# Whole-tile turns, sample-memory products on two row halves and memories decayed ahead by POOL in a hybrid recurrent decoder step

## The chip, the cores and the metric

The kernel runs on one core of one Trainium2 chip. The metric is device time in microseconds for one launch, which computes the whole two-layer trunk; the figure for a kernel is the median of its runs. One more execution is recorded by the hardware profiler, and all rows below come from that one.

## What is computed

Each of two layers is: a SwiGLU feed-forward half step with a layer norm, one input projection, two recurrent mixers side by side, an output projection with a layer norm, and a second feed-forward half step. A prompt of 256 tokens and 8 samples of 8 tokens share the weights; only the samples come with states. Cut to the state updates that the change touches:

```python
def step(S, inp):                       # RWKV-7, 8 heads of 64x64, per token
    r_t, w_t, k_t, v_t, kk_t, a_t = inp
    sa = jnp.einsum('bhvk,bhk->bhv', S, -kk_t)
    S = (S * w_t[:, :, None, :] + sa[..., None] * (kk_t * a_t)[:, :, None, :]
         + v_t[..., None] * k_t[:, :, None, :])
    return S, jnp.einsum('bhvk,bhk->bhv', S, r_t)
...
C = dec[..., None, None] * C + jnp.einsum('bhs,bhsd,bhse->bhde', ws, kc, vc)   # mLSTM, 4 heads of 128x128, per chunk
n = dec[..., None] * n + jnp.einsum('bhs,bhsd->bhd', ws, kc)
```

## The kernel before

Everything is kept transposed: features on the 128 partitions, the 320 tokens (two tiles of 128 prompt tokens and tile 2 of 64 sample tokens) along the free dimension. The projections and feed-forward parts split each fp32 weight and activation in a high and a low fp32r part and make three products of them (`three_passes`, L2047 to L2049); weights come by SP's queue into four slots `raw`, ScalarE makes the high part (L2337) and VectorE the low one (L2538). Engines meet only by semaphores, and the order of the work on each engine is written out by hand.

The mixers stand between the input and the output projection. `tensor_mixers` first turns the mLSTM keys and values to tokens on partitions, tile by tile (`keys_of_tile`, L535; `values_of_tile`, L544; ScalarE copies them with `copy_keys`, L1049, and `copy_values`, L1057), between the RWKV score products (L755). Then comes the growth loop of 27 steps (`for n in range(NSTEP)`), which inverts a triangular matrix for each of 5 RWKV chunks in up to 6 levels. A step, called by its n below, is: a product on TensorE (L725), a mask on VectorE (L1660), the two growth products of the step before (L737, L740), a copy on ScalarE (L1133). Everything else of the mixers is hung on these steps by lists of numbers:

- `SIDE_AT`: the side jobs of `side`, which all go through bank 7 and are each copied out by ScalarE in `copy_side` before the next may start: the last rows, the values of 5 chunks (L665), the keys of 5 chunks in two halves each (L674, 10 sides at steps 9 to 18), three products for the right-hand sides (L681), the convolution ends (L685), and four turns of wkv memories (L694, steps 23 to 26).
- `NUM_AT`, `SCORES_AT`, `HEAD_AT`: the mLSTM's products of a tile; head statistics on VectorE at steps 17, 18 and 20 for tiles 0 and 1, at 24 to 26 for tile 2 (L1471 to L1510).
- `LEFT_AT`: the left-over jobs in banks 4 to 6. The eight C jobs are the new sample memories, each the half (4 samples) of one head: TensorE multiplies keys of tile 2 with the values masked by sample (L630, 512 columns), and VectorE multiplies the old memory by its decay and adds the product, four instructions per job (L1522). They stand in pairs at steps 20, 21, 23 and 24. Their masked values come from POOL (L1828), in two buffers. The sample memories lie in `raw` and leave on SP's queue (L2029) before the output projection's weights may come in.

POOL's queue in this stretch is, in order: identity added to the scores (L1859), the decayed keys `bkh` (L1864, L1867), zeroing of `qm` (L1873), the load of wkv memories (L1877), decay matrices (L1881), masked values (L1828), memory terms (L1836), and two groups of stores. Behind the loop stands `recurrence`, four chunks in sequence.

The pattern of a left-over and a side job in the code:

```python
if kind == "C":
    pe.wait_ge(vmask_ready.sem, vmask_ready.by(L, i // 2 + 1))
    last = pe.matmul(b[:, :], kt[0:TS, 2, i // 2, :], vmask[(i // 2) % 2][:, 4 * (i % 2):4 * (i % 2) + 4, :],
                     start=True, stop=True)
```

## Time and profile before

| | |
|---|---|
| median of 3 runs | 1550.63 us (1549.57 to 1556.33) |
| span of the profiled execution | 1551.5 us |
| VectorE busy | 982.2 us (63%) |
| ScalarE busy | 696.5 us (45%) |
| POOL busy | 375.1 us (24%) |
| mean granted TensorE clock | 0.975 |
| growth loop and recurrence, layer 1 | about 389 to 500 us |
| the same, layer 2 | about 1147 to 1265 us |

A granted clock of 1.00 is 2.4 GHz, 0.50 is 1.2 GHz. PE is TensorE, DVE VectorE, ACT ScalarE. A matmul in fp32 leaves more than one record. Neighbouring records of one line are merged in a timeline, so that a group's duration runs from its first start to its last end, with an end that may overlap the next group's start. L12 is line 12 of the kernel before.

### The profile page before, as it was taken

How to read it: one execution, taken by the hardware profiler on the slowest of the kernel's cores; microseconds unless marked ns; L12 is line 12 of the kernel's file. 1: busy time of each engine (PE TensorE's matmuls, PEld its weight loads, DVE VectorE, ACT ScalarE, POOL GpSimd, SP SyncE). 2: the span in 40 equal slices, each digit the busy share in tenths (PEclk: the TensorE clock that was granted, in tenths of full speed). 3: DMA queues.
4: the chain of work that ended last, by engine and by line, in shares of the span. 5: the costliest groups of instructions: out<-in, count | busy, mean ns of one | idle time of the engine just before them, and what ended most of it. 6: DMA issues, size and time to landing. Idle time of an engine off the chain costs nothing.

```text
span 1551.5 us, 34978 instructions
## 1 busy us (share of the span) xinstructions
PE 1489.7 (96%) x13874; PEld 1434.4 (92%) x13874; DVE 982.2 (63%) x1571; ACT 696.5 (45%) x1198; POOL 375.1 (24%) x395
## 2 busy tenths in 40 slices
PE   7999998999889999999999999989988999999995
PEld 7999998999778999999999999989988789999995
DVE  4444445587276787776577775466944667877644
ACT  4333334755545543334343334367563355333332
POOL 4222472011241422221322221200142304222100
PEclk9999999999998999999999999999999799999998
DMA  8555542553123655444545545534430434545451
GB/s 216 149 149 149 165 149 69 136 137 96 32 60 91 167 157 154 137 148 136 169 138 147 149 149 164 149 96 109 109 85 3 120 86 143 170 138 164 144 163 34
DMA packets 318846, 198.89 MB, mean 128 GB/s; under 512 B 7696, under 2 KB 303664, under 8 KB 318736
## 3 DMA queue, kind: packets, MB, share of 16 engines
q1 hardware_dynamic: 315120, 190.69, 42.2%
q0 software_dynamic: 3616, 6.62, 2.0%
q8 instruction: 82, 1.34, 0.4%
q14 instruction: 28, 0.23, 0.0%
HBM read 188.50 MB, written 8.78 MB: 127 GB/s over the span
## 4 chain that ended last, share of the span: by engine, by line
PE 83%; DVE 8%; ACT 5%; DVEq 2%; issue 2%; DMA 0%; ACTq 0%; SPq 0%
PE bank L2047 23%; PE bank L2049 23%; PE bank L2048 23%; DVE wlo L2538 2%; PE bank L2134 1%; PE bank L630 1%; PE bank L725 1%; ACT whi L2337 1%; DVE rlo L2569 1%; PE bank L2139 1%; PE bank L455 1%; ACT z L1133 1%; PE bank L740 1%; PE bank L755 1%; PE bank L737 1%
## 5 line engine op out<-in xcount | busy, mean ns | idle before, releaser
L2337 ACT ACTIVATE whi<-raw 128x1024 fp32r<-128x1024 f32 x340 | 358.8, 1060 | 470.3 <-PE bank L2049 453.9
L2538 DVE TENSOR_TENSOR wlo<-raw,whi 128x1024 fp32r<-128x1024 f32 x340 | 421.7, 1244 | 228.5 <-ACT whi L2337 227.7
L2047 PE MATMUL bank<-rhi,whi 128*128 128x322 f32 x984 | 306.5, 311 | 0.0
L2049 PE MATMUL bank<-rhi,wlo 128*128 128x322 f32 x984 | 305.9, 311 | 0.0
L2048 PE MATMUL bank<-rlo,whi 128*128 128x322 f32 x984 | 304.8, 310 | 0.0
L2047 PE MATMUL bank<-xh,whi 128*128 128x320 f32 x912 | 285.3, 313 | 5.8 <-DVE xl L2712 3.5
L2048 PE MATMUL bank<-xl,whi 128*128 128x320 f32 x912 | 282.2, 309 | 0.0
L2049 PE MATMUL bank<-xh,wlo 128*128 128x320 f32 x912 | 282.2, 309 | 0.0
L2807 POOL TENSOR_TENSOR hl<-scratch,hh 128x320 f32 x88 | 146.8, 1668 | 496.4 <-DVE scratch L2659 379.7
L2047 PE MATMUL bank<-hh,whi 128*128 128x320 f32 (+1 forms) x704 | 218.4, 310 | 0.5 <-DVE wlo L2538 0.5
L2048 PE MATMUL bank<-hl,whi 128*128 128x320 f32 (+1 forms) x704 | 217.4, 309 | 0.0
L2049 PE MATMUL bank<-hh,wlo 128*128 128x320 f32 (+1 forms) x704 | 217.4, 309 | 0.0
L2048 PEld LDWEIGHTS bank<-rlo,whi 128*128 128x128 f32 x984 | 186.5, 189 | 0.0
L2047 PEld LDWEIGHTS bank<-rhi,whi 128*128 128x128 f32 x984 | 185.5, 189 | 0.0
L2049 PEld LDWEIGHTS bank<-rhi,wlo 128*128 128x128 f32 x984 | 185.5, 189 | 0.0
L2047 PEld LDWEIGHTS bank<-xh,whi 128*128 128x128 f32 x912 | 172.1, 189 | 10.9 <-issue 7.2
L2048 PEld LDWEIGHTS bank<-xl,whi 128*128 128x128 f32 x912 | 172.2, 189 | 0.5
L2049 PEld LDWEIGHTS bank<-xh,wlo 128*128 128x128 f32 x912 | 172.1, 189 | 0.0
L2047 PEld LDWEIGHTS bank<-hh,whi 128*128 128x128 f32 x704 | 132.3, 188 | 1.4 <-issue 1.0
L2048 PEld LDWEIGHTS bank<-hl,whi 128*128 128x128 f32 x704 | 132.4, 188 | 0.2
L2049 PEld LDWEIGHTS bank<-hh,wlo 128*128 128x128 f32 x704 | 132.4, 188 | 0.0
L2640 DVE TENSOR_TENSOR scratch<-bank,scratch 128x322 f32<-128x322 f32 x132 | 64.9, 491 | 70.8 <-PE bank L2049 63.1
(411 smaller groups left out, 1960.3 us busy)
## 6 DMA issues: line engine op xcount, KB each, us to landing
raw<-in_ffn_wg SPq DMA_DIRECT2D x88, 512.0 KB, 3.8
raw<-in_ffn_wu SPq DMA_DIRECT2D x88, 512.0 KB, 3.8
raw<-in_ffn_wd SPq DMA_DIRECT2D x88, 512.0 KB, 3.7
raw<-in_w_in SPq DMA_DIRECT2D x60, 512.0 KB, 3.8
raw<-in_w_out SPq DMA_DIRECT2D x16, 512.0 KB, 6.4
raw<-in_state_C SPq DMA_DIRECT2D x8, 512.0 KB, 6.2
out_s_C<-raw SPq DMA_DIRECT2D x8, 512.0 KB, 3.8
ring<-in_state_wkv POOLq DMA_DIRECT2D x2, 1024.0 KB, 8.3
```

What stands on the lines that cost most here:

```text
L455: return pe.matmul(out, src, ident[0:rows, 0:rows], start=True, stop=True)
L630: last = pe.matmul(b[:, :], kt[0:TS, 2, i // 2, :], vmask[(i // 2) % 2][:, 4 * (i % 2):4 * (i % 2) + 4, :], start=True, stop=True)
L725: last = pe.matmul(bank[n % 2][PART[1 - q], j * CH:(j + 1) * CH], ati[part, c, j, :], xi(q, c, j), start=True, stop=True)
L737: pe.matmul(bank[2 + q][PART[q], j * CH:(j + 1) * CH], xti(q, c, j), t1[PART[1 - q], c, j, :], start=True, stop=True)
L740: last = pe.matmul(bank[2 + q][PART[1 - q], j * CH:(j + 1) * CH], t1[PART[1 - q], c, j, :], xti(q, c, j), start=True, stop=True)
L2047: pe.matmul(out, w_hi, hi, start=start, stop=False)
L2048: pe.matmul(out, w_hi, lo, start=False, stop=False)
L2049: return pe.matmul(out, w_lo, hi, start=False, stop=stop)
L2337: act.activation(whi[:, slot, :], raw[:, slot, :], ACT.Copy).then_inc(hi_ready.sem, 1)
L2538: dve.tensor_tensor(wlo[:, slot, :], raw[:, slot, :], whi[:, slot, :].bitcast(F32), ALU.subtract).then_inc(lo_ready.sem, 1)
L2640: dve.tensor_tensor(scaled, bank_of(L, f, d)[:, 0:T + 2], root, ALU.mult)
L2807: pool.tensor_tensor(at(hl), hval[:, k % 2, :], at(hh).bitcast(F32), ALU.subtract).then_inc(hl_done.sem, 1)
```

## The change

- The second head of each pair gets a second copy of its keys, values and gate column of tile 2, on partitions 64 to 127. The C jobs are reordered so that the two of a step belong to the two heads of a pair; one uses rows 0 to 63 of TensorE, the other rows 64 to 127.
- The old sample memories are multiplied by their decay on POOL (`decayed_memory`, eight instructions), and VectorE only adds the product, one instruction per C job, behind a new wait on `memory_decayed`. The masked values are made for two heads at once, so that two POOL instructions stay of four.
- The keys of a chunk are turned as full tiles, four transpositions for a chunk, in one side instead of two; POOL therefore writes the two kinds of decayed keys in swapped places on the upper partitions, in eight instructions instead of three.
- The wkv memories are loaded with two heads beside each other, in four DMAs of POOL's queue instead of one, and turned by four transpositions of full tiles per side instead of sixteen products of 64x64.
- With 5 sides fewer, `SIDE_AT` puts the keys at steps 9, 10, 11, 13, 14, the products for right-hand sides at 15 to 17, the ends at 19, and the wkv memories at 20, 21, 23 and 24.

The diff, with context cut:

```diff
...
         tail = area(6144, P, rows=(SB + 1) * NRW, of=ring)
-        wkv_rows = area(6144, SB, NJ, NA, of=ring)
+        wkv_rows = area(6144, SB, NJ // 2, P, of=ring)
         C0 = raw[:, :, :].rearrange("p h (b e) -> p h b e", b=SB)
...
         hsq = area(0, 2 * HB * DK, of=spare)
-        vmask = [area(1536, SB, DK, rows=TS, of=spare), area(15304, SB, DK, rows=TS)]
+        vmask = [area(1536, SB, DK, of=spare), area(15304, SB, DK)]
...
         h_ready = signal("h_ready", 2)
-        vmask_ready = signal("vmask_ready", HB)
+        memory_decayed = signal("memory_decayed", 2 * HB)
+        vmask_ready = signal("vmask_ready", HB // 2)
         left_mm = signal("left_mm", 13)
...
         x_copied = signal("x_copied", NSTEP)
-        side_mm = signal("side_mm", 24)
-        side_copied = signal("side_copied", 24)
+        side_mm = signal("side_mm", 19)
+        side_copied = signal("side_copied", 19)
         tail_out = signal("tail_out", 32)
         ends_left = signal("ends_left", 48)
-        wkv_in = signal("wkv_in", 16)
+        wkv_in = signal("wkv_in", 64)
         samples_mm = signal("samples_mm", 4)
...
                     last = turn(pe, bank[4][0:rows, (n * 3 + q) * HB:(n * 3 + q + 1) * HB], row[:, q, at:at + rows])
+            for h in range(0, HB, 2):
+                own = 8 * HB + h
+                last = pe.matmul(bank[4][PART[1], own:own + 1], row[:, 2, 2 * P:T], sel[:, h + 1, 0:1],
+                                 start=True, stop=True)
             last.then_inc(cols_turned.sem, 1)
...
                 last = turn(pe, bank[4 + n][0:rows, h * DK:(h + 1) * DK], qk[:, HB + h, at:at + rows])
+                if n == 2 and h % 2 == 0:
+                    last = turn(pe, bank[4 + n][PART[1], h * DK:(h + 1) * DK], qk[:, HB + h + 1, at:at + rows])
             last.then_inc(kv_turned.sem, 1)
...
         def values_of_tile(pe, L, n):
...
                                     ident[:, :])
+                if n == 2 and h % 2 == 0:
+                    last = pe.matmul(bank[5][PART[1], h * DK:(h + 1) * DK], mv[:, h + 1, at:at + rows], ident[:, :],
+                                     start=True, stop=True)
             last.then_inc(kv_turned.sem, 1)
...
         def tile_scores(pe, L, n):
...
             if kind == "C":
-                pe.wait_ge(vmask_ready.sem, vmask_ready.by(L, i // 2 + 1))
-                last = pe.matmul(b[:, :], kt[0:TS, 2, i // 2, :], vmask[(i // 2) % 2][:, 4 * (i % 2):4 * (i % 2) + 4, :],
+                g, half, q = i // 4, i // 2 % 2, i % 2
+                pe.wait_ge(vmask_ready.sem, vmask_ready.by(L, g + 1))
+                last = pe.matmul(b[:, :], kt[PART[q], 2, 2 * g, :], vmask[g][PART[q], 4 * half:4 * half + 4, :],
                                  start=True, stop=True)
...
-        VALUES, KEYS, RVS, ENDS, MEMS = 1, 1 + NCH, 1 + 3 * NCH, 4 + 3 * NCH, 5 + 3 * NCH
+        VALUES, KEYS, RVS, ENDS, MEMS = 1, 1 + NCH, 1 + 2 * NCH, 4 + 2 * NCH, 5 + 2 * NCH
         NSIDE = MEMS + SB // 2
-        SIDE_AT = [*range(KEYS), *range(KEYS + 3, NSIDE + 3)]
+        SIDE_AT = [*range(KEYS), 9, 10, 11, 13, 14, 15, 16, 17, 19, 20, 21, 23, 24]
+        assert len(SIDE_AT) == NSIDE
         RV = ((0, 1), (2, 3), (NPC,))
...
         def side(pe, L, k):
...
                     pe.wait_ge(bkh_ready.sem, bkh_ready.by(L, 1))
-                c, q = (k - KEYS) // 2, (k - KEYS) % 2
                 for j in range(NJ):
-                    for kind in range(2):
-                        last = pe.matmul(b[PART[q ^ kind], j * NA:(j + 1) * NA], bkh[PART[q], j, c, kind, :],
-                                         ident[PART[q], PART[q]], start=True, stop=True)
+                    last = pe.transpose(b[:, j * P:(j + 1) * P],
+                                        bkh[:, j, k - KEYS, :, :].rearrange("p s t -> p (s t)"), ident[:, :])
             elif k < ENDS:
...
                 if k == MEMS:
-                    pe.wait_ge(wkv_in.sem, wkv_in.by(L, 16))
+                    pe.wait_ge(wkv_in.sem, wkv_in.by(L, 64))
                 for i in range(2):
-                    for j in range(NJ):
-                        for part in PART:
-                            at = (i * NJ + j) * NA
-                            last = pe.matmul(b[part, at:at + NA], wkv_rows[part, 2 * (k - MEMS) + i, j, :],
-                                             ident[part, part], start=True, stop=True)
+                    for jj in range(NJ // 2):
+                        at = (i * NJ // 2 + jj) * P
+                        last = pe.transpose(b[:, at:at + P], wkv_rows[:, 2 * (k - MEMS) + i, jj, :], ident[:, :])
             last.then_inc(side_mm.sem, 1)
...
                 last = act.activation(cols[0:rows, n, 1:3, :], src[:, 1:3, :], ACT.Exp)
+            last = act.activation(cols[PART[1], 2, 2, 0:HB:2], bank[4][PART[1], 8 * HB:9 * HB:2], ACT.Exp)
             last.then_inc(cols_ready.sem, 1)
...
                                       scale=cols[0:rows, n, 2, h:h + 1])
+            if n == 2:
+                for h in range(0, HB, 2):
+                    last = act.activation(kt[PART[1], 2, h, :], bank[6][PART[1], h * DK:(h + 1) * DK], ACT.Identity,
+                                          scale=cols[PART[1], 2, 2, h:h + 1])
             last.then_inc(kv_ready.sem, 1)
...
         def copy_values(act, L, n):
...
             act.wait_ge(kv_turned.sem, kv_turned.by(L, NTT + n + 1))
+            if n == 2:
+                act.activation(va[PART[1], 2, 0:HB:2, 0:DK],
+                               bank[5][PART[1], :].rearrange("p (h d) -> p h d", h=HB)[:, 0:HB:2, :], ACT.Copy)
             act.activation(va[0:rows, n, :, 0:DK], bank[(7, 4, 5)[n]][0:rows, :].rearrange("p (h d) -> p h d", h=HB),
...
             elif k < RVS:
-                c, q = (k - KEYS) // 2, (k - KEYS) % 2
-                last = act.activation(bkt[c][:, :, q, :], heads4(b), ACT.Copy)
+                last = act.activation(bkt[k - KEYS][:, :, :, :].rearrange("p j q n -> p (j q n)"), b[:, :], ACT.Copy)
             elif k < ENDS:
...
             if kind == "C":
-                h, half = i // 2, i % 2
-                for k in range(4):
-                    s = 4 * half + k
-                    at = h * TS + s * ST + ST - 1
-                    last = dve.scalar_tensor_tensor(out=C0[:, h, s, :], in0=C0[:, h, s, :], scalar=rexp[:, at:at + 1],
-                                                    in1=b[:, k * DK:(k + 1) * DK], op0=ALU.mult, op1=ALU.add)
+                h, half = 2 * (i // 4) + i % 2, i // 2 % 2
+                own = C0[:, h, 4 * half:4 * half + 4, :].rearrange("p b e -> p (b e)")
+                dve.wait_ge(memory_decayed.sem, memory_decayed.by(L, i + 1))
+                last = dve.tensor_tensor(own, own, b[:, :], ALU.add)
             elif kind == "H":
...
-        def masked_values(pool, L, h):
-
-            values = va[0:TS, 2, h, 0:DK].rearrange("t (o e) -> t o e", o=1)
-            own = bmask[0:TS, :].rearrange("t (b o) -> t b o", o=1)
-            pool.tensor_tensor(vmask[h % 2], bcast(values, 1, SB), bcast(own, 2, DK),
+        def masked_values(pool, L, g):
+
+            values = va[:, 2, 2 * g, 0:DK].rearrange("t (o e) -> t o e", o=1)
+            own = bmask[:, :].rearrange("t (b o) -> t b o", o=1)
+            pool.tensor_tensor(vmask[g], bcast(values, 1, SB), bcast(own, 2, DK),
                                ALU.mult).then_inc(vmask_ready.sem, 1)
+
+        def decayed_memory(pool, L, i):
+
+            h, half = 2 * (i // 4) + i % 2, i // 2 % 2
+            own = C0[:, h, 4 * half:4 * half + 4, :]
+            at = h * TS + 4 * half * ST
+            decay_ = rexp[:, at:at + 4 * ST].rearrange("p (b t) -> p b t", t=ST)[:, :, ST - 1:ST]
+            pool.tensor_tensor(own, own, bcast(decay_, 2, DK), ALU.mult).then_inc(memory_decayed.sem, 1)
...
         def memory_term(pool, L, j):
...
             two = lambda t: t.rearrange("p j c s t -> p j c (s t)")
-            pool.tensor_tensor(two(bkh[:, :, 0:NPC, :, :]), two(bk[:, :, 0:NPC, :, :]),
-                               bcast(dlast[:, :, 0:NPC].rearrange("p j (c o) -> p j c o", o=1), 3, 2 * CH), ALU.mult)
             for s in range(2):
-                last = pool.tensor_tensor(
-                    seqs(bkh[:, :, NPC, s, :]), seqs(bk[:, :, NPC, s, :]),
-                    bcast(dlast[:, :, NPC:NPC + SB].rearrange("p j (c o) -> p j c o", o=1), 3, ST), ALU.mult)
+                pool.tensor_tensor(bkh[PART[0], :, 0:NPC, s, :], bk[PART[0], :, 0:NPC, s, :],
+                                   bcast(dlast[PART[0], :, 0:NPC].rearrange("p j (c o) -> p j c o", o=1), 3, CH),
+                                   ALU.mult)
+                pool.tensor_tensor(bkh[PART[1], :, 0:NPC, s, :], bk[PART[1], :, 0:NPC, 1 - s, :],
+                                   bcast(dlast[PART[1], :, 0:NPC].rearrange("p j (c o) -> p j c o", o=1), 3, CH),
+                                   ALU.mult)
+                for q, part in enumerate(PART):
+                    last = pool.tensor_tensor(
+                        seqs(bkh[part, :, NPC, s, :]), seqs(bk[part, :, NPC, s ^ q, :]),
+                        bcast(dlast[part, :, NPC:NPC + SB].rearrange("p j (c o) -> p j c o", o=1), 3, ST), ALU.mult)
             last.then_inc(bkh_ready.sem, 1)
...
             carry(pool)
-            dma(wkv_rows[:, :, :, :].rearrange("p b j k -> p (b j) k"),
-                lay(I["state_wkv"]).rearrange("l b (j q) v k -> (q v) (l b j) k", q=2)).then_inc(wkv_in.sem, 16)
+            for a, part in enumerate(PART):
+                for q in range(2):
+                    src = lay(I["state_wkv"]).rearrange("l b (j h) v k -> v (l b j) h k", h=4)
+                    dma(wkv_rows[part, :, :, q * NA:(q + 1) * NA].rearrange("p b j k -> p (b j) k"),
+                        src[:, :, 2 * a + q, :]).then_inc(wkv_in.sem, 16)
             pool.wait_ge(tile_mm.sem, tile_mm.by(L, NTT))
...
             pool.wait_ge(num_mm.sem, num_mm.by(L, NTT))
+            decayed_memory(pool, L, 0)
+            decayed_memory(pool, L, 1)
             masked_values(pool, L, 1)
-            pool.wait_ge(left_mm.sem, left_mm.by(L, 2))
-            masked_values(pool, L, 2)
-            pool.wait_ge(left_mm.sem, left_mm.by(L, 4))
-            masked_values(pool, L, 3)
+            for i in range(2, 2 * HB):
+                decayed_memory(pool, L, i)
             pool.drain()
...
                 for h in range(HB):
-                    sp.wait_ge(left_done.sem, left_done.by(L, LEFT.index(("C", 2 * h + 1)) + 1))
+                    sp.wait_ge(left_done.sem, left_done.by(L, LEFT.index(("C", 4 * (h // 2) + 2 + h % 2)) + 1))
                     sp.dma_start(lay(O["s_C"])[:, :, h, :, :].rearrange("l b d e -> d (l b) e"),
```

## Rows read from the trace of the kernel before

**Rows 1.** The page: busy time, share of the span and instructions of each engine.

```profile
PE 1489.7 (96%) x13874; PEld 1434.4 (92%) x13874; DVE 982.2 (63%) x1571; ACT 696.5 (45%) x1198; POOL 375.1 (24%) x395
```

**Rows 2.** The page: shares by engine of the chain that ended last.

```profile
PE 83%; DVE 8%; ACT 5%; DVEq 2%; issue 2%; DMA 0%; ACTq 0%; SPq 0%
```

**Rows 3.** Windows: stretch, length, PE, PEld, DVE, ACT, POOL busy, clock, DMA, GB/s.

```profile
391.00:433.00 42.00, 36.07 (x984) 33.46 (x984) 12.45 (x38) 21.75 (x64) 11.82 (x10) 0.92 0.13 29
433.00:443.00 10.00, 7.18 (x262) 6.49 (x259) 9.39 (x21) 2.76 (x8) 4.73 (x2) 1.00 0.01 3
443.00:466.00 23.00, 21.46 (x482) 15.54 (x474) 17.21 (x60) 10.75 (x27) 9.64 (x7) 1.00 0.35 99
...
1191.00:1201.00 10.00, 7.26 (x256) 6.57 (x252) 9.04 (x21) 3.06 (x9) 4.94 (x2) 1.00 0.02 6
1201.00:1231.00 30.00, 29.39 (x482) 20.73 (x482) 17.84 (x60) 10.58 (x27) 8.24 (x7) 0.72 0.26 75
```

**Rows 4.** Timeline of TensorE: start, duration, line, records, idle before.

```profile
281.88 1.35 PE L487 MATMUL bank<-scratch 64*128 64x320 f32 x8
...
354.64 2.16 PE L455 MATMUL bank<-ident,scratch 32*128 32x32 f32 x20
...
381.14 1.09 PE L455 MATMUL bank<-ident,scratch 128*64 128x128 f32 x8
382.15 0.66 PE L544 MATMUL bank<-ident,scratch 128*128 128x128 f32 x4
...
432.50 0.68 PE L674 MATMUL bank<-ident,spare 64*64 64x64 f32 x16
...
442.77 0.27 PE L737 MATMUL bank<-spare,z 64*64 64x64 f32 x2 [2.82 <-DVE spare L1660]
...
443.30 1.10 PE L681 MATMUL bank<-scratch 64*64 64x64 f32 x32
444.90 1.98 PE L630 MATMUL bank<-spare,ring 64*128 64x512 f32 x4 [0.50 <-ACT ring L1083]
...
453.54 1.10 PE L694 MATMUL bank<-ident,ring 64*64 64x64 f32 x32
```

**Rows 5.** The chain of waits, first layer, ahead of the growth loop: start, us, what.

```profile
385.47 0.57 PE bank L544 x4
386.06 0.60 ACT ring L1057
```

**Rows 6.** Timeline of ScalarE.

```profile
382.26 1.13 ACT L1049 ACTIVATE ring<-bank,scratch 64x128 f32<-64x128 f32 x4 [0.31 <-PE bank L455]
...
444.07 0.77 ACT L1083 ACTIVATE ring<-bank 64x258 f32<-64x258 f32 x2
```

**Rows 7.** Timeline of POOL.

```profile
390.88 3.61 POOL L1864 TENSOR_TENSOR spare<-scratch 128x2048 f32<-128x2048 f32 x1 [0.35 <-issue]
394.45 1.22 POOL L1867 TENSOR_TENSOR spare<-scratch 128x256 f32<-128x256 f32 x2
...
439.00 2.88 POOL L1828 TENSOR_TENSOR scratch<-ring,bmask 64x1024 f32<-64x1024 f32 x1
...
452.59 2.05 POOL L1836 TENSOR_TENSOR scratch<-scratch,bmask 128x512 f32<-128x512 f32 x2 [0.24 <-ACT scratch L1120]
```

**Rows 8.** One line, L674: ns min/median/max, first and last start in us.

```profile
L674 PE MATMUL bank<-ident,spare x320: 218/218/365, 406.7 to 1194.5; 64*64 64x64 f32 x160
```

**Rows 9.** Timeline of VectorE.

```profile
435.96 1.17 DVE L1482 TENSOR_TENSOR ring<-ring,scratch 128x1024 f32<-128x1024 f32 x1
...
437.55 2.57 DVE L1492 TENSOR_TENSOR spare<-ring 128x1024 f32<-128x1024 f32 x1
...
448.06 2.15 DVE L1522 SCALAR_TENSOR_TENSOR raw<-raw,ring,bank 128x128 f32<-128x128 f32 x8
...
452.86 1.28 DVE L1528 TENSOR_TENSOR scratch<-bank,scratch 128x512 f32<-128x512 f32 x2
```

**Rows 10.** The chain of waits, second layer, step 20.

```profile
1203.44 3.75 PE bank L630 x4
```

## The prediction

> **What bounds the kernel now.** I read the page first: TensorE is busy for 96% of the span [rows 1] and holds 83% of the chain that ended last [rows 2]. The reader should see that most of this is the projections and feed-forward layers, which the change leaves alone. The change lives in the mixer stretch, some 120 us per layer, so I cut that stretch into windows [rows 3]. From 391 to 433 us TensorE is busy 36 of 42 us at a granted clock of 0.92: steps 5 to 17 of the growth loop. From 433 to 443 VectorE is busy 9.39 of 10 us and TensorE 7.18: VectorE's head means and squares set the pace. From 443 to 466 both are loaded (21.5 and 17.2 of 23 us). The second layer is the same but for its last part, which takes 30 us at a clock of 0.72 where the first takes 23 us at 1.00. So what an edit is worth depends on its step; I went through it by the timelines of the four engines [rows 4, 6, 7, 9] and by the chain of waits [rows 5, 10] and asked at each step which wait ends last.
>
> **The change, part by part.** One record of an ordinary fp32 matmul counts half of that matmul; a transposition of a full tile is one record only [rows 4]: eight records for four products at L455, four for four transpositions at L544.
>
> (1) Second copy of keys, values and gate columns. Before the growth loop TensorE turns keys of tile 2 (four products of 64 tokens, 1.01 us from the start of L455 to that of L544 [rows 4]), so 0.25 us each. Two more for keys and two more for values are 1.0 us, and they stand in the unbroken TensorE work ahead of the last values copy, which the chain runs through [rows 5]. Behind it ScalarE has one more copy of 64 rows before its table load; ScalarE copies of 64 rows by 256 to 258 take 0.38 (two L1083 in 0.77) [rows 6]. The two added key copies cost 0.28 each (four L1049 in 1.13) [rows 6] and are hidden by ScalarE's waits for values; uncovered they would be 0.56. The two gate-column products lie in the input projection, TensorE-bound: the twenty records of such small products take 2.16 us (L455 at 354.64) [rows 4], four are 0.43. Sum: 1.0 + 0.38 + 0.43 = 1.8 us **lost** per layer.
>
> (2) POOL's decayed keys. One instruction over 2048 elements takes 3.61 us and two small ones 1.22 [rows 7]. By its elements each of the four new ones over 1024 takes 1.8, so 7.2, and the small ones double to 2.4: 4.8 us later, at 400.5 instead of 395.7. The first turn of keys starts at 406.7 [rows 8], so 6 us of cover remain. Behind them on POOL's queue stand the zeroing of qm and now four issues of wkv memories instead of one; they are needed at steps 16 and 20, the latter at 443 (L681) [rows 4], over 35 us later. I cost this at nothing; if the cover were gone, up to 5 us per layer.
>
> (3) Turns of keys. Ten sides of eight products (0.68 for one, L674) become five sides of four transpositions (0.66, L544) [rows 4]; some 0.1 of each is a tail that overlaps the next work. TensorE saves five times 0.57, 2.9 us, but nearly none on the path. The removed sides leave steps 12, 14 and 18, where TensorE waits for ScalarE's and VectorE's weights of a tile anyway; step 15 gets a product side (sixteen products, L681, 1.10 [rows 4]) in place of a turn, and it does stand ahead of the next product: 0.4 us, and 0.6 at the clock of 0.92 and lower that this window has: 0.6 us **lost** per layer. The like at step 16 is hidden behind VectorE.
>
> (4) Turns of wkv memories. Four sides of sixteen products (1.10, L694) become four transpositions each (0.66, L544) [rows 4]: 0.44 saved four times, two of them where TensorE sets the pace.
>
> (5) Products into the sample memories. A pair takes 1.98 us [rows 4] (L630, four records of 0.495). In the changed kernel the two of a pair use different row halves and banks. The row that shows such a pattern is L487: eight records of 320 columns with alternating row halves in 1.35 us [rows 4]. At 0.495 x 320/512 = 0.31 each they would need 2.5 us one after another, so they ran two at a time. I take 1.0 us for a pair, bounds 1.0 and 1.98.
>
> (6) VectorE. Eight instructions of a pair take 2.15 us (L1522); two additions over 512 elements from PSUM and SBUF take 1.28 (L1528, same form) [rows 9]: 0.87 saved per pair.
>
> (7) POOL's decays. Eight over 128x512 at about 1.02 (two L1836 in 2.05 [rows 7]), and two masks fewer. From about 438, where its masks begin now (the second runs from 439.00), POOL has two decays, one mask of 1.8 (half of L1864's 3.61 for half its elements) and six decays without a wait: 10.0 us, until some 448.5. The first pair's products end at 444.9 + 1.0, when two decays have long been done; each later pair comes 2 us or more behind it, as long as POOL takes for two. So no wait on memory_decayed is expected. But POOL is now busy through 438 to 448.5, and the rows show that the two engines hold each other up: L1482 takes 1.17 us, L1492 of the same size, beside a POOL mask, 2.57, and the mask beside it 2.88 [rows 7, 9]. The additions of (6) read one operand from PSUM, as L1522 did, and no L1522 row is stretched. I take 0.5 us lost at the first head scaling, half of one POOL instruction; L1492 might win back up to 1.4 if POOL starts behind it, which I leave out. Bounds: -1.4 and +2 per layer. The Trainium skill, GPSIMD Engine Reference, the table at its head, says that POOL shares its SBUF interfaces with VectorE and contends with VectorE instructions that have two SBUF inputs; by that rule, the trace agrees (2.57 against 1.17).
>
> Steps 20 to 24 of the first layer, from the sum of these: step 20 starts from ScalarE's table load and is VectorE-bound: -0.87 + 0.5 = -0.4. Step 21: VectorE, -0.85. Step 23: TensorE-bound, 1.98 + 1.10 become 1.0 + 0.66, then VectorE binds: -1.2. Step 24: VectorE (head means, then the pair), -0.85. Steps 22, 25, 26: nothing. Together **-3.3 us**. In the second layer the first two pairs run at half clock, 3.75 us for the first on the chain [rows 10]: a pair saves 1.85 there. Two of them are -3.7, and -1.5 remains of the other steps: **-5.2 us**.
>
> (8) Changes of tile shape. Turns with full tiles stand between products of 64x64; before they had the same shape. The Trainium skill, TensorEngine Tiling (Array Packing), Key Properties, says that a change of tiling mode drains TensorE. This rule speaks against the change. No row isolates its price. Without that rule a bound from rows: the 64x64 work before L544 and behind it leaves no gap in the windows where TensorE is full, so I take nothing, and as upper end for the nine sides the 0.1 us tail of each, 0.9 us per layer.
>
> **Sum.** Layer 1: +1.8 +0.6 -3.3 = -0.9. Layer 2: +1.8 +0.6 -5.2 = -2.8. Together -3.7 us. The profiled execution's span is 1551.5, 0.9 above the median 1550.63; against the median I forecast 1546.9.
>
> **Rivals.** *Half clock in the first layer too* (the slower side). VectorE-bound steps 17 to 19 leave TensorE idle for 2.82 us (L737) [rows 4]; the change takes turns out of just these steps, so it idles longer. In the first layer the clock stayed, in the second it fell behind such a gap [rows 3]. The first layer's 23 us would become as the second's 30: 6.8 lost, 1.9 of it given back by cheaper pairs, 4.9 net: 1551.8. (Full clock is 2.4 GHz, half is 1.2.) It decides once it costs over 3.7 us, if the fall comes before step 22. For it: the same program has both cases in one execution. Against: the gap grows by 1 or 2 us only. Chance 0.22.
> *Clock kept in the second layer*: the mirror image, 1546.9 - 4.9 = 1542.0; chance 0.15.
> *The pairs don't overlap*: then (5) gives nothing, steps 23 and 24 lose 0.4, the second layer 3.7: 1551.0. Against it stands L487; chance 0.08.
> *POOL's decays hold VectorE up*: each POOL instruction of 1.02 us can stand ahead of the two head products and scalings of tiles 0 and 1, at most 2 us a layer: 1550.9; chance 0.12. By the skill's rule on shared interfaces it is these instructions, with two SBUF inputs, that would be longer.
> *The forecast*: 0.43.
>
> **Numbers.** The clock rivals and the bounds of (7) and (8) set the range, 1540.5 to 1555. A measurement here can tell about 0.5%, 7.75 us, from no change: faster means below 1542.9, slower above 1558.4. Faster 0.20 (most of the clock-kept case, with part of the forecast's lower tail); slower 0.06 (clock fallen and POOL's holding together, or an unseen drop later in the mixer); the same 0.74.
>
> **What would show it.** Right: L630 pairs of about 1.0 us; L1522 gone, additions of 0.64; L674-like turns as records of 128x128, four each; the last values copy 1.4 us later against the start of the stretch; POOL's last decay ended before the third pair of additions; the first layer's stretch from step 19 to 26 about 20 us instead of 23.3. Wrong: a VectorE wait on POOL before an addition; TensorE waiting for wkv rows at step 20 or for bkh at step 9; a pair of 1.5 to 2 us; a low clock at a place where it was full, which would move the total by more than all my terms together.

## The result

The changed kernel takes 1562.87 us (median of 7 runs, 1558.99 to 1566.81), the kernel before 1553.25 beside it (7 runs, 1549.57 to 1557.27): ratio 1.0065, 95% interval 1.0047 to 1.0083. It is 0.65% **slower**; the forecast was 1546.9 us, 0.2% faster, with a range that ended at 1555.

The page after, as [rows 1, 2]: busy time by engine, then the shares of the chain that ended last.

```profile
span 1559.3 us, 34012 instructions
PE 1485.8 (95%) x13394; PEld 1428.9 (92%) x13394; DVE 986.7 (63%) x1523; ACT 696.0 (45%) x1196; POOL 395.1 (25%) x423
PE 84%; DVE 7%; ACT 5%; DVEq 2%; issue 1%; DMA 0%; SPq 0%; ACTq 0%
```

TensorE does 4 us less work and the span is 7.8 longer. VectorE has 48 instructions fewer and is 4.5 us busier: some of them got longer. POOL has 20 us more. From the first score product to the first weight split of the output projection (`wlo`) the two layers take 119.8 and 126.6 us before, 126.1 and 127.7 after: +7.4 of the 7.8. By stage, from the places of the growth masks:

| stage | layer 1, us | layer 2, us |
|---|---|---|
| ahead of the first mask behind the score products | +1.33 | +1.34 |
| from there to the mask of step 18 | +0.02 | +2.55 |
| mask of step 18 to mask of step 19 (step 19 below) | +2.07 | +2.21 |
| mask of step 19 to mask of step 26 | +0.39 | -6.12 |
| from there to `wlo` (the recurrence) | +2.52 | +1.16 |

Windows of after, as [rows 3] (stretch, length, PE, PEld, DVE, ACT, POOL busy, granted clock, DMA, GB/s):

```profile
391.00:433.00 42.00, 35.12 (x955) 31.85 (x957) 12.34 (x37) 23.48 (x64) 20.00 (x20) 0.96 0.15 30
433.00:443.00 10.00, 7.13 (x225) 6.01 (x216) 9.54 (x19) 2.86 (x10) 4.86 (x4) 1.00 0.04 10
443.00:446.00 3.00, 0.00 (x0) 0.00 (x0) 2.85 (x4) 0.00 (x0) 3.00 (x4) 0.71 0.06 16
446.00:470.00 24.00, 19.13 (x321) 13.24 (x321) 17.17 (x37) 9.41 (x23) 8.78 (x9) 0.78 0.28 79
470.00:492.00 22.00, 20.98 (x380) 19.48 (x384) 8.93 (x23) 7.38 (x19) 5.40 (x8) 0.50 0.43 122
```

Two things are new. TensorE does nothing at all from 443 to 446 us while VectorE and POOL are both full; and the clock, which before was 1.00 from 443 to 466, is here 0.71 in that gap (it falls inside it), 0.78 from 446 to 470 and 0.50 until 492.

**The gap.** VectorE before, the statistics ahead of the mask of step 19, which follow L1492 (2.57 us) [rows 9] and L1494:

```profile
441.48 0.41 DVE L1496 SCALAR_TENSOR_TENSOR scratch<-scratch 128x8 f32<-128x8 f32 x1
441.97 0.17 DVE L1498 TENSOR_TENSOR scratch<-scratch 128x8 f32<-128x8 f32 x1
442.22 0.17 DVE L1500 TENSOR_SCALAR scratch<-scratch 128x8 f32<-128x8 f32 x1
```

The same five instructions after, and the masks behind them:

```profile
439.04 2.10 DVE L1507 TENSOR_TENSOR spare<-ring 128x1024 f32<-128x1024 f32 x1
441.22 1.22 DVE L1509 TENSOR_REDUCE scratch<-spare 128x8 f32<-128x1024 f32 x1
442.51 1.42 DVE L1511 SCALAR_TENSOR_TENSOR scratch<-scratch 128x8 f32<-128x8 f32 x1
444.00 0.93 DVE L1513 TENSOR_TENSOR scratch<-scratch 128x8 f32<-128x8 f32 x1
445.01 0.93 DVE L1515 TENSOR_SCALAR scratch<-scratch 128x8 f32<-128x8 f32 x1
445.86 0.74 DVE L1673 TENSOR_TENSOR spare<-bank,lvmask 128x256 f32<-128x256 f32 x2
...
451.23 1.99 DVE L1525 TENSOR_TENSOR ring<-ring,scratch 128x1024 f32<-128x1024 f32 x1
```

And POOL and TensorE of after:

```profile
439.01 3.04 POOL L1850 TENSOR_TENSOR raw<-raw,ring 128x512 f32<-128x512 f32 x2 [5.14 <-PE bank L619]
442.01 1.89 POOL L1841 TENSOR_TENSOR scratch<-ring,bmask 128x1024 f32<-128x1024 f32 x1
443.87 6.07 POOL L1850 TENSOR_TENSOR raw<-raw,ring 128x512 f32<-128x512 f32 x6
450.09 2.04 POOL L1857 TENSOR_TENSOR scratch<-scratch,bmask 128x512 f32<-128x512 f32 x2 [0.16 <-issue]
```

```profile
446.32 0.37 PE L745 MATMUL bank<-spare,z 64*64 64x64 f32 x2 [5.47 <-DVE spare L1673]
```

Two instructions over 8 elements a partition take 0.93 us in place of 0.17, nearly the length of one decay (six in 6.07). Their ends fall on the ends of POOL's instructions: L1511 ends at 443.93, where POOL's mask makes way for a decay (443.87), L1513 at 444.93 and L1515 at 445.94, and decays follow each other about every 1.01 us from 443.87 on. Against before, L1507 is 0.47 shorter, L1511 is 1.01 longer, L1513 and L1515 0.76 each: +2.06, and from one growth mask (L1673) to the next this step takes 7.16 instead of 5.09 us, +2.07 (7.15 instead of 4.94 in the second layer). TensorE waits for those masks for 5.47 us where it waited 2.82 [rows 4].

**The half clock.** By windows of 1 us in the two mixer stretches, TensorE is at 0.50 in before from 410, 427 and 468 us, the last until 482, and in the second layer also from 1202 to 1219: 51 us together. In after it is so from 427, 444 and 468, the last until 492: 75 us together.

Such a sum is of one execution, and it scatters. In e4 and e12 below, whose instructions are those of after as far as the loop's step 20, it is 14 us between 376 and 438 us, in after itself 3. A difference of some 10 us between two kernels is therefore not read from one trace alone. The mean clock of all runs of a kernel says more. The kernel before, run more than 130 times beside the experiments, took 1557.9 us on average in the 19 runs at a mean clock of 0.972 and 1549.6 in the 10 at 0.978: 18.6 us less of half clock over the whole program go with 8.3 us less time, 0.45 us for each. Where TensorE is not what the others wait for, half clock costs less (e4 below).

### The profile page after: what moved, and what is told of

Its sections match the earlier page's. It is cut to its first block, busy times and chain, and to the rows that moved or that the text cites. A ratio compares the mean times of both kernels' runs of the same rounds, so it can differ in the third digit from the quotient of the medians.

```text
span 1559.3 us, 34012 instructions
## 1 busy us (share of the span) xinstructions
PE 1485.8 (95%) x13394; PEld 1428.9 (92%) x13394; DVE 986.7 (63%) x1523; ACT 696.0 (45%) x1196; POOL 395.1 (25%) x423
## 3 DMA queue, kind: packets, MB, share of 16 engines
q8 instruction: 78, 1.28, 0.4%
## 4 chain that ended last, share of the span: by engine, by line
PE 84%; DVE 7%; ACT 5%; DVEq 2%; issue 1%; DMA 0%; SPq 0%; ACTq 0%
PE bank L2076 23%; PE bank L2078 23%; PE bank L2077 23%; DVE wlo L2567 2%; PE bank L2163 1%; ACT whi L2366 1%; DVE rlo L2598 1%; PE bank L733 1%; PE bank L456 1%; PE bank L2168 1%; ACT z L1148 1%; PE bank L641 1%; PE bank L745 1%; PE bank L748 1%; PE bank L788 1%
```

## The experiments

Theory A: POOL's decays hold up VectorE's statistics; taken away, the loss goes. Theory B: TensorE's clock falls behind idle time, and part of the loss comes from that. A filler below is a TensorE product whose result nobody reads. The runs are in this table, each ratio against runs of the kernel before on the same chip (so it is not the quotient of the two medians); mean clock is that of all runs of the kernel, which over the whole program makes 3.1 us of half clock for each 0.001; half clock is the sum over 1 us windows of 2 x (1 - granted clock) in both stretches, step 19 the distance from its growth mask back to the one before it, first and second layer, these two from one profiled execution each.

| kernel | median us | ratio to before | interval | mean clock | half clock us | step 19 us |
|---|---|---|---|---|---|---|
| before | 1553.25 | 1 | | 0.974 | 51 | 5.09, 4.94 |
| after | 1562.87 | 1.0065 | 1.0047 to 1.0083 | 0.968 | 75 | 7.16, 7.15 |
| e1 decays late | 1553.97 | 0.9998 | 0.9983 to 1.0012 | 0.970 | 72 | 3.49, 3.80 |
| e2 decays on VectorE | 1558.03 | 1.0019 | 1.0001 to 1.0038 | 0.970 | 68 | 5.61, 5.26 |
| e3 turns only | 1561.98 | 1.0042 | 1.0026 to 1.0059 | 0.967 | 82 | 5.22, 4.87 |
| e4 filler in after | 1564.28 | 1.0058 | 1.0037 to 1.0079 | 0.970 | 72 | 7.16, 7.16 |
| e5 products only | 1554.48 | 1.0007 | 0.9989 to 1.0026 | 0.975 | 44 | 7.61, 7.62 |
| e6 filler in before | 1547.29 | 0.9961 | 0.9942 to 0.9980 | 0.978 | 41 | 5.09, 4.94 |
| e7 e1, second term late | 1553.38 | 1.0001 | 0.9983 to 1.0019 | 0.970 | 65 | 3.49, 3.79 |
| e8 turns, old places | 1552.29 | 0.9998 | 0.9985 to 1.0011 | 0.971 | 75 | 5.05, 4.63 |
| e9 e7, later places | 1555.66 | 1.0021 | 1.0008 to 1.0035 | 0.969 | 79 | 3.84, 4.20 |
| e10 products, late decays | 1549.24 | 0.9974 | 0.9958 to 0.9990 | 0.978 | 51 | 4.84, 5.15 |
| e11 e10 and filler | 1549.98 | 0.9987 | 0.9971 to 1.0003 | 0.977 | 55 | 4.84, 5.15 |
| e12 after, filler at end | 1560.48 | 1.0040 | 1.0024 to 1.0057 | 0.976 | 55 | 7.15, 7.15 |
| e13 before, two fillers | 1542.07 | 0.9932 | 0.9911 to 0.9954 | 0.987 | 17 | 5.08, 4.94 |
| e14 e10, two fillers | 1548.00 | 0.9960 | 0.9944 to 0.9976 | 0.983 | 38 | 4.84, 5.16 |
| e15 e7, two fillers | 1548.77 | 0.9978 | 0.9963 to 0.9993 | 0.983 | 24 | 3.49, 3.80 |
| e16 before, small fillers | 1543.70 | 0.9917 | 0.9896 to 0.9939 | 0.984 | 31 | 5.09, 4.95 |

### Decays behind the statistics (e1, e7), and on VectorE (e2)

```diff
# e1, and e7
             pool.wait_ge(num_mm.sem, num_mm.by(L, NTT))
+            pool.wait_ge(hvar_ready.sem, hvar_ready.by(L, 1))
             decayed_memory(pool, L, 0)
# e7 beside it
-            pool.wait_ge(left_mm.sem, left_mm.by(L, 10))
+            pool.wait_ge(left_done.sem, left_done.by(L, 10))
# e2
-                last = dve.tensor_tensor(own, own, b[:, :], ALU.add)
+                (four scalar_tensor_tensor per job, as in the kernel before; no decays on POOL)
```

> The changed kernel with one more wait: POOL starts its decays of the sample memories only when VectorE has finished the head statistics of tiles 0 and 1 (signal hvar_ready). Theory A (collision): in the changed kernel POOL's back-to-back decays hold up the short VectorE instructions of step 18 (1.42, 0.93 and 0.93 us where the kernel before has 0.41, 0.17, 0.17), and t1 of step 18 to t1 of step 19 takes 7.15 us against 5.1. By A this distance falls back to 5.1 or below in both layers, TensorE's gap falls from 5.4 to about 3.3 us, and the time falls by at least 4 us: ratio to the kernel before 1.001 to 1.004. Theory B (clock): what costs is the low clock behind a TensorE gap, and the gap is mostly the removed TensorE work; then the gap stays above the 2.8 us of before, the clock still falls behind it in both layers, and the ratio stays at 1.005 to 1.007. Theory C (added work ahead of the loop and product sides at step 15): nothing to do with POOL, ratio stays at 1.0065.

> The changed kernel with the decays back on VectorE (four instructions a job, as before), everything else changed. Theory A (collision): step 18 to 19 back at 5.1 us; the later steps lose the 0.87 us per pair that the additions saved, but win back the stretched statistics of tile 2; ratio 1.000 to 1.003. Theory B (clock): gap still longer than before, ratio about 1.005. Theory C (added copies, product side at step 15): ratio about 1.005, with +1.4 and +0.6 us per layer ahead of step 17 unchanged.

> As e1 (decays start behind the statistics of tiles 0 and 1), and POOL's second memory term waits until VectorE has made the last memory addition, so that it doesn't run beside the statistics of tile 2 in step 24. Theory A (collision): step 25 falls from 5.36 us to about 3.8, as VectorE's instructions there sum up without being held; 1 to 1.5 us per layer, ratio 0.998 against 0.9998 for e1. Theory B (clock): the shorter steps are given back by TensorE at low clock behind them: ratio as e1, 1.000.

e1 takes back the whole 0.65%. VectorE in e1, in the same place, with POOL's first decay at 443.83:

```profile
440.44 1.22 DVE L1507 TENSOR_TENSOR spare<-ring 128x1024 f32<-128x1024 f32 x1
441.73 1.22 DVE L1509 TENSOR_REDUCE scratch<-spare 128x8 f32<-128x1024 f32 x1
443.02 0.17 DVE L1511 SCALAR_TENSOR_TENSOR scratch<-scratch 128x8 f32<-128x8 f32 x1
443.27 0.17 DVE L1513 TENSOR_TENSOR scratch<-scratch 128x8 f32<-128x8 f32 x1
443.51 0.17 DVE L1515 TENSOR_SCALAR scratch<-scratch 128x8 f32<-128x8 f32 x1
```

All five have their lone length, L1507 too, which in before is held up by a POOL mask. Nothing but one wait on POOL was added, so the collision is the cause of these 3.67 us (7.16 to 3.49). The wait holds back POOL's second mask too, which stands behind the first two decays. So 2.07 of the 3.67 are what after had lost against before, and 1.6 are a holding that before has as well: e1 gains more than it undoes (its forecast by Theory A was 1.001 to 1.004), and that its ratio is 1 does not mean that the decays were the whole loss. Over both layers after lost 4.3 us in step 19, of 9.6. The expensive instructions are the three over 8 elements: none is long, each waits for a POOL instruction. e2 leaves POOL's early mask in place and lies between: L1507 takes 2.94 us, L1511 0.56, the head scaling 1.23 where after has 1.99. e7 takes the same collision out of step 25 too, 5.37 to 3.79 us, and its ratio does not move beyond its interval: step 26 takes 3.56 us in place of 2.83, and TensorE stands 2.88 us ahead of the last growth products.

### Each half of the change (e5, e3, e8)

```diff
# e5: after, with before's turns and SIDE_AT.  e3: before, with after's turns and SIDE_AT.  e8: e3 and
-        SIDE_AT = [*range(KEYS), 9, 10, 11, 13, 14, 15, 16, 17, 19, 20, 21, 23, 24]
+        SIDE_AT = [*range(KEYS), 9, 10, 11, 13, 14, 19, 20, 21, 22, 23, 24, 25, 26]
```

> The kernel before with the whole-tile turns of keys and wkv memories alone (new order of side jobs, swapped writes of POOL, four DMAs); no second copies, no row halves, decays on VectorE. Theory A (collision): masks of POOL meet VectorE as before; only +0.6 us at step 15 and -0.4 to -0.9 us at the late turns per layer: ratio 0.998 to 1.000. Theory B (clock): TensorE has 3 us less work per layer around step 18, its gap grows from 2.8 to about 3.5 to 4.5 us, the clock falls in both layers, ratio 1.002 to 1.004. Theory C says the turns' side at step 15 costs: at most 1.001.

> The kernel before with the sample-memory products alone: second copies of keys and values, two heads on the two row halves, decays ahead by POOL, one addition; turns and side jobs as before. Theory A (collision): step 19 takes about 7.1 us instead of 5.1 and step 25 about 5.4, and 1.3 us per layer are added ahead of step 5: with the first layer's pairs saving little, ratio 1.003 to 1.006. Theory B (clock): TensorE keeps its side jobs in steps 19 to 26, so the low clock behind step 24 is shorter than the 24 us of the changed kernel in the first layer, and the ratio is 1.000 to 1.002.

> The kernel before with the whole-tile turns alone, as in e3 (1.0042), but the side jobs behind the keys stay at their old steps: products for right-hand sides at 19 to 21, ends at 22, wkv turns at 23 to 26. Theory D (what cost e3 was the moving of TensorE work ahead of the gap): 1.1 us per layer come back at steps 16 and 17, and the low clock behind the gap in the first layer becomes shorter or goes: ratio 0.999 to 1.001. Rival: the transpositions themselves, with their changes of tile shape, cost: then steps 10 to 14 or 24 to 26 are longer than before and the ratio stays near 1.004.

e3 and e8 do the same work; eight side jobs stand at other steps. e3 is at 1.0042, e8 at 0.9998, and the intervals are apart. The windows from 445 to 462 us show where; first e3, then e8:

```profile
445.00:462.00 17.00, 16.63 (x165) 10.12 (x162) 7.94 (x23) 5.30 (x12) 5.84 (x4) 0.51 0.22 63
```

```profile
445.00:462.00 17.00, 15.93 (x291) 10.29 (x290) 12.29 (x41) 8.05 (x21) 6.89 (x4) 1.00 0.29 81
```

TensorE is equally busy, with half the instructions in e3, at 0.51. Ahead of that it had stood 3.55 us in e3 (ahead of the growth products behind the masks of steps 19 and 20) and 2.28 and 0.57 in e8. From the mask of step 19 to that of step 26 e3 takes 30.03 and 26.32 us, e8 22.97 and 22.63. So whole-tile turns have no price of their own that shows (0.9998), and the price of their places is for the most part the clock: 0.967 against 0.971 in the mean, though by the half-clock sums the two differ by only 7 us. e8's half clock from 435 to 443 lies where VectorE sets the pace, e3's from 444 to 462 where TensorE is busy throughout. e5, with a step 19 of 7.6 us, is level with before, which Theory A alone does not give; its profiled execution (44 us of half clock, 1550.12 us) is faster than its median by 4.4, so the 44 against 51 says little, and its mean clock is that of before. What it gains are the steps 20 to 26, 21.47 and 21.48 us against 23.28 and 30.13. The two halves, 1.0042 and 1.0007, add to 1.0049 where the whole is 1.0065; the intervals allow that.

### Products whose result nobody reads (e4, e6)

```diff
                     product(pe, L, n)
+                    if n == 20:
+                        for _ in range(6):      # e6: range(3), in the kernel before
+                            pe.matmul(bank[5][:, 0:6 * CH], ident[:, :], lvmask[...], start=True, stop=True)
```

> The changed kernel with six extra TensorE products of 384 columns into an unused part of bank 5 at step 20, where TensorE sits idle for 5.4 us; their result is not used. They take about 0.74 us each, 4.4 in all, so they fit the gap. Theory B (clock): the granted clock stays at 2.4 GHz behind the gap, the first two pairs of memory products and the turns between take half as long, and the time falls by 2 to 6 us, ratio 1.002 to 1.005. Theory A (collision): the gap itself stays, the time falls by at most 1 to 2 us. If the clock falls all the same, ratio unchanged at 1.0065.

> The kernel before with three extra TensorE products of 384 columns at step 20 (about 0.74 us each, unused), in the gap of 2.8 us that TensorE has there. Theory B (clock is bought by TensorE's gaps): the second layer's low clock of 17 us behind that gap does not come or is shorter, and the time falls by 3 to 7 us, ratio 0.996 to 0.998. If the low clock comes whatever TensorE does in the gap: ratio 0.999 to 1.001, and the low stretches only change their places.

e6 only adds work, and it is 0.39% faster. Its first layer is as before; in the second the steps 22 to 24 take 2.40, 1.53 and 3.74 us where before has 5.96, 4.22 and 4.69. In windows, first e6, then (two windows) e13, which has more fillers, against the 0.72 of [rows 3] for the like stretch:

```profile
1201.00:1231.00 30.00, 27.89 (x569) 21.12 (x566) 20.99 (x67) 12.26 (x31) 15.19 (x14) 0.91 0.46 130
```

```profile
468.00:482.00 14.00, 13.18 (x349) 11.04 (x348) 7.24 (x18) 6.42 (x17) 4.88 (x7) 1.00 0.64 174
...
1201.00:1231.00 30.00, 30.00 (x620) 21.94 (x622) 21.40 (x68) 10.97 (x28) 15.05 (x14) 1.00 0.56 152
```

In after the same idea gave nothing (1.0058 beside 1.0065). The six products took 4.14 us and left 1.41 of the 5.47 us idle; the clock stayed at 1.00 until 452 and was low until 456, where in after it is low from 444 to 455. Yet from the mask of step 19 to that of step 26 the first layer takes 23.39 us, and 23.67 in after: this fall, by itself, cost after 0.3 us. The way to the mask of step 21 is as long at either clock (8.48 and 8.47 us); in after VectorE there stands 3.79 us for ScalarE (L1521 for L1112).

### Late places with late decays, and the products alone with them (e9, e10, e11)

```diff
# e9: e7 and
+        SIDE_AT = [*range(KEYS), 9, 10, 11, 13, 14, 18, 19, 20, 21, 22, 23, 24, 25]
# e10: e5 with e7's two waits.   e11: e10 and three products at step 20, as in e6
```

> The changed kernel with GpSimd's decays behind VectorE's statistics and the second memory term late (as in e7_decays_and_term_late), and eight side turns moved from steps 15 to 17 and 19 to 24 to steps 18 to 25. Theory A (only the collision of GpSimd with VectorE costs time; it is gone in e7 at 1.0001): the turns' places are worth nothing, 1.000, steps 16 and 17 a micro-second shorter together and the later ones as much longer. Theory B (a part of the loss is TensorE's clock behind gaps; the two turns-only kernels differ by 0.44% by the places alone): the late places give back the same here, 0.996, and the time at the half clock in both mixer stretches falls from 65 us to about 50.

> The changed kernel without its whole-tile turns (turns and their places as in the kernel before; the pair products, the decays on GpSimd and the one addition stay), with the decays behind VectorE's statistics and the second memory term late. Theory A: the same part without the late decays is at 1.0007 with a step 19 of 7.6 us in both layers; step 19 falls to about 3.5, which is 3.8 us a layer over the stretch at most, so 1551.5 - 7 = 1544.5, 0.9955. Theory B: as in the second layer of the changed kernel, time that is won in front of the gap comes back as half clock behind it; the half-clock time goes up from 44 us, and the ratio is 0.998 to 1.000.

> As e10_products_late_decays, with three TensorE products of 384 columns ahead of step 21 whose result nobody reads (the same three that made the kernel before faster, 0.9961). Theory A: TensorE works 0.5 us more in each layer, so the ratio is that of e10 or up to 0.0006 above it. Theory B: the products keep the clock up behind the gap of step 20, mostly in the second layer, where the three of them were worth 6 us in the kernel before: 0.002 to 0.004 below e10.

e9 missed both ways: late places, worth 0.44% between e3 and e8, gave nothing here (1.0021 beside the 1.0001 of e7; the intervals overlap, so a loss is not shown either). "Later is better" is therefore no rule. e10 is the first version with parts of the change that is faster than both kernels, 0.9974, but by little more than half of what Theory A gave it: step 19 falls to 4.84 and not to 3.5, since its statistics (L1511 at 2.56 us) meet POOL's first mask, and half clock is 51 us, as in before. e11's filler did nothing that the intervals can tell from e10.

### Fillers behind the loop (e12, e13, e16) and with the change's parts (e14, e15)

```diff
+            idle_products(pe, 5)      # e13, e14: 3; e15: 6; e16: 1
             grow(pe, L, NSTEP - 1)
+            idle_products(pe, 2)      # e16: 1
             recurrence(pe, L)
```

`idle_products(pe, k)` makes k of the products of 384 columns, into bank 1. e12 is after with these alone; e13 and e16 are the kernel before, e14 is e10 and e15 is e7, each with the three products at step 20 too.

> The changed kernel with seven TensorE products of 384 columns whose result nobody reads: five ahead of the last half of the growth loop (grow of step 26), where TensorE stands for 2.14 us in the first layer, and two behind it, where it stands for 0.87 us. At some 0.37 us each they fit into the idle time. Theory B (the recurrence is 2.5 us longer in the first layer than before because TensorE is at the half clock from 468 to 492 us, where before it was from 468 to 482, and it is so because TensorE stands 2.0 and 2.1 us in the last steps where it stood 1.1 us): the half clock ends by about 480 or does not come, the stretch from the last growth step to the first output projection falls from 34.8 to 32 us or less, and the ratio is 1.000 to 1.004. Rival: the idle time is not what sets the clock, or other places take it over as with e4_filler: 34.8 us again and 1.0065; if the products are in the way, up to 1.008.

> The kernel before with the three products ahead of step 21 (0.9961 as e6_before_filler) and, beside them, three ahead of grow of step 26 (idle 1.09 us in the first layer) and two behind it (idle 0.87 us). Theory B: the half clock from 468 to 482 us, and that from 1226 to 1239 in the second layer, shrink or go, which is worth up to 6 us a stretch: 0.990 to 0.994. Rival: no further gain, 0.996.

> As e10_products_late_decays (pairs on two row halves, decays on GpSimd behind VectorE's statistics, one addition; the turns as before: 0.9974) with the fillers of e13_before_two_fillers: three products ahead of step 21, three ahead of grow of step 26, two behind it. If what this half of the change wins is real once TensorE stays at full clock: the kernel before with the same fillers is at 0.9932; VectorE has 0.87 us less per pair in steps 20, 21 and 24 and TensorE 0.9 less per pair in step 23, while the copies ahead of the loop cost 1.3 us and step 19 at most nothing, so 1 to 2 us a layer: 0.991 to 0.992. If it only moved idle time: 0.993 or above, with half clock back at another place.

> The whole change with late decays and a late second memory term (as e7_decays_and_term_late, 1.0001) and fillers: three products ahead of step 21, six ahead of grow of step 26 (idle 2.88 us in that kernel), two behind it. Theory B: half clock behind the last growth steps goes, the recurrence falls from 33 or 34 us to 30 or 31, and the ratio is 0.994 to 0.997. If whole-tile turns take so much work out of steps 18 to 26 that the clock falls elsewhere (two turns-only kernels of ours had it behind step 19): 0.998 to 1.001.

> As e13_before_two_fillers (0.9932), with one product ahead of grow of step 26 and one behind it in place of three and two. One such product takes 0.73 us at full clock (six records in 2.20), so three and two of them were longer than the idle times of 1.09 and 0.87 us and held the loop's end up by 1.1 + 0.6 = 1.7 us a layer; one and one fit. If filling the idle time is what keeps the clock: full clock stays, 1.7 us less a layer, 0.991. If it needed that much more work (a rival: the clock answers to how much the products add, not to the idle time they fill): the half clock behind 468 us comes back at least in part, 0.994 to 0.996.

They go against the idle time at the end of the loop. TensorE there, with its idle time in brackets, first before, then after:

```profile
466.05 0.68 PE L740 MATMUL bank<-z,spare 64*64 64x64 f32 x16 [1.09 <-DVE spare L1660]
467.60 0.68 PE L854 MATMUL bank<-scratch,z 64*64 64x64 f32 x16 [0.87 <-ACT z L1133]
```

```profile
467.18 0.68 PE L748 MATMUL bank<-z,spare 64*64 64x64 f32 x16 [2.02 <-DVE spare L1673]
470.00 1.12 PE L748 MATMUL bank<-z,spare 64*64 64x64 f32 x16 [2.14 <-DVE spare L1673]
471.98 1.12 PE L862 MATMUL bank<-scratch,z 64*64 64x64 f32 x16 [0.87 <-ACT z L1148]
```

e12 in the first layer: five products and then two more.

```profile
472.02 5.19 PE L917 MATMUL bank<-lvmask,ident 128*128 128x384 f32 x10
477.75 1.56 PE L917 MATMUL bank<-lvmask,ident 128*128 128x384 f32 x4
```

They take longer than the idle time they were put into; I had taken one record for a product (0.37 us), and a product is two. Nevertheless the stretch from the last growth mask to `wlo` falls from 34.79 to 30.56 us in the first layer, with the clock full from 476 on. In the second it rises from 33.04 to 35.20, with half clock from 1247 to 1258, and the ratio goes to 1.0040. e13 has both fillers on the kernel before: 0.9932, half clock 17 us in place of 51, and that stretch 28.62 and 30.39 where before has 32.27 and 31.88. e16, with products that fit the idle time better, is level with it (0.9917; the intervals overlap): some half clock returned and less work was in the way. e13 and e16 are the fastest of all.

e14 and e15 do not come near e13. e15's span is 1546.9 against 1540.2. By the mean clock of all runs (0.983 against 0.987) it has 12 us more half clock, worth at most 6 of these 6.7 us; by the two mixer stretches of its trace it has 7 us more, worth at most 3.5. So with its decays out of the way the change still gains nothing, and costs some 1 to 3 us at a like clock; that this is the 1.3 us ahead of the loop in each layer would fit, and is not shown.

## Point by point

**Right.** (1) The loop's first mask comes 1.33 and 1.34 us later against the stretch's start (forecast 1.4 without the gate columns); the extra copy of values is there, 0.38 us as costed, ahead of the table load:

```profile
387.17 0.38 ACT L1071 ACTIVATE ring<-bank 64x256 f32<-64x256 f32 x1 [1.91 <-PE bank L551]
387.56 0.59 ACT L1073 ACTIVATE ring<-bank 64x512 f32<-64x512 f32 x1
...
388.17 1.28 ACT L1078 ACT_TABLE_LOAD   x1
```

The 0.43 of the input projection did not show. (2) POOL's keys end at 402.0 and delay nobody. (4, 5, 6) Turns, pairs and additions have their forecast lengths: a pair 1.1 us (forecast 1.0, 1.98 before), two additions 1.29 (1.28), a turn 0.66:

```profile
458.39 0.66 PE L703 MATMUL bank<-ident,ring 128*128 128x128 f32 x4
...
458.98 1.13 PE L641 MATMUL bank<-scratch,ring 64*128 64x512 f32 x4
...
460.14 1.28 DVE L1536 TENSOR_TENSOR raw<-raw,bank 128x512 f32<-128x512 f32 x2 [1.53 <-PE bank L641]
```

So the row halves do work side by side, by the pattern read from L487 [rows 4]. (8) e8, whole turns at their old places, is at 0.9998: the change of tile shape has no price that shows.

**(7) failed: the term was mis-sized.** I took 0.5 us at the head scaling. The scaling lost 0.76 (1.99 against 1.23 in before), and step 19 lost 2.07: together 2.8 us in a layer, above my upper bound of 2. The mechanism had been read correctly from L1492 beside a mask [rows 7, 9], and was a rival at 0.12 too. What went wrong is what I counted: the two large head products and scalings, once each. The short instructions between them, 0.17 us each and three in a row ahead of the masks TensorE waits for, were costed at nothing, and they lost 2.53 us, while L1507 won 0.47 back. The row that should have warned me is L1496 of before, 0.41 us where its neighbours of the same size take 0.17, beside the same POOL mask. The Trainium skill, GPSIMD Engine Reference, section Specifications, names as those that contend VectorE instructions with two SBUF inputs or in a 2-port perf mode. By the first half the trace agrees for L1507, L1511 and L1513. L1515 and L1494 have one tensor input and were held too (0.93 us; 1.03 beside the memory term of step 24); which perf mode they ran in no row tells. L1509, a reduction with one input, kept its 1.22 us beside the same POOL instructions.

**The sum of steps 20 to 26 failed.** From the mask of step 19 to that of step 26 the first layer takes 23.67 us where 20.0 was forecast (before: 23.28), the second 24.01 (forecast 24.9; before 30.13). The second is right in size for another reason than mine: the half clock of 1202 to 1219 is shorter (1212 to 1222). What pairs and additions are worth at full clock is read from e10, first layer, which has before's turns: 22.24 us, 1.04 less than before and not 3.3. (e5, with the early decays, takes 21.47 there, 1.81 less; its last step is 0.64 shorter, as its second memory term is not held back.) Step by step e10 has -0.17, -0.87, +0.72, -0.29, -0.81, +0.38 for the masks of steps 21 to 26. The -0.87 of an addition is there at step 22 and nearly at 25, but step 21 gives 0.69 of it back to a scaling beside POOL (L1529 1.92 us against 1.23 in before). What step 22 wins step 23 loses: TensorE, with the shorter pair, waits for the additions in front of it before it may write the second half of the next pair, and comes late to step 23. I had taken each step's saving as if the step before it had not moved:

```profile
452.84 1.12 PE L641 MATMUL bank<-spare,ring 64*128 64x512 f32 x2 [0.72 <-DVE raw L1540]
```

**(3) was low.** Steps 16 and 17 together are 1.13 us longer in the first layer and 1.87 in the second, against 0.6 at step 15. What else the second layer loses ahead of the mask of step 18 lies in steps 10 and 11, +1.78, where the clock is low for 8 us (1174 to 1182) and in before for 4; e12, the same work there, does not have it. I count that as scatter.

**The recurrence was costed at nothing.** It is 2.52 and 1.16 us longer. e12 shows for the first layer that this is the half clock and not the recurrence's own work, of which nothing is changed: with the clock full from 476 on the stretch takes 30.56 us. The rows on the clock that I worked from end at 466 us [rows 3]; in before too it falls at 468, until 482.

**The rivals.** Two of them came true together, which I had down as the case for "slower" and given 0.06: the clock fell in the first layer at step 19, and the decays held VectorE up. I had priced the clock's fall by the gap that the removed turns leave ("1 or 2 us"), and the decays apart from it; the held-up statistics made the gap 2.65 us longer. But that this longer gap made the clock fall is not shown: e1, where TensorE stands 1.81 us there and 0.85 behind it, and e3, without any decay on POOL, have the fall too (445 to 452, 444 to 462). And the price I gave it, 4.9 us, it did not have: e4 puts it at 0.3. The low clock that cost this layer time was the one in the recurrence.

**What stays open.** Of the 9.6 us between the medians (7.8 between the profiled executions), the 4.3 in step 19 have a cause that e1 shows, and 2.7 ahead of the loop are the added work of (1); how much of the clock's part is the change's doing, and where it falls, is argued and not shown. Idle time of TensorE alone does not tell it: e9 has the later places and no higher a clock, e4 and e11 put products into the gap of step 20 for nothing, and e10, e11, e12 and e14 are all at half clock near 412 to 418 us, where after itself is not.

## What to carry over

When work goes to POOL, list every VectorE instruction that it will run beside, the short ones first: each can wait for a whole POOL instruction (0.17 to 0.93 us here; the reduction and the masks from PSUM did not), and the chain of three lost more (2.53 us) than the one long operation (0.88). Where TensorE stands for microseconds in a stretch, moving its work may cost more than the work itself (e3 and e8); first look at the granted clock behind each gap, and try a few idle products, which made the kernel before 0.4 to 0.8% faster. A low clock is worth what the steps in it lose, not its length. Price a saving on two alternating engines by the pair of steps, not by the step.

## What the runs showed of the hardware

- A VectorE instruction over 8 elements a partition took 0.17 us alone and 0.93 beside POOL's instructions over 512 elements (about 1.01 each), twice in a row. Two growth masks (L1673), which read PSUM and SBUF, kept their length beside the same POOL instructions (0.74 us, 0.75 in before), and so did a reduction with one SBUF input (L1509, 1.22).
- Two fp32 products of 64 rows by 512 columns (four records), one on each row half, took 1.13 us in place of 1.98 on one half, and 2.08 at half clock.
- Extra TensorE work made a kernel faster: 0.9961 with three products a layer, 0.9932 with eight and 0.9917 with five. The Trainium skill, TensorE: Matmul & The Clock Gate, section What's actually happening, says that the granted clock follows how busy the engine has been; by that these three agree, since the mean clock went from 0.974 to 0.978, 0.987 and 0.984; in after (e4) and e10 (e11) the like products gave no gain.
